# A four-layer streaming trunk on one core: order of work where a mixer joins its FFN, two squares on ScalarE, sums of squares inside the second gate unit

## What is computed

```python
for i in range(DEPTH):                       # DEPTH = 4
    h = _rmsnorm(x, attn_norm[i])
    if i % 3 == 0:   x = x + stick_breaking_mixer(h, ...)
    elif i % 3 == 1: x = x + mla_mixer(h, ...)
    else:            x = x + swa_sink_mixer(h, ...)
    x = x + swiglu_ffn(_rmsnorm(x, ffn_norm[i]), w_gate, w_up, w_down)
return _rmsnorm(x, final_norm)

def swiglu_ffn(h, w_gate, w_up, w_down):     # FFN_HIDDEN = 2816
    return (jax.nn.silu(h @ w_gate) * (h @ w_up)) @ w_down
```

## Time and profile before

| | |
|---|---|
| median of 3 runs | 1195.81 us (1195.05 to 1196.33) |
| profiled execution, own time | 1196.22 us |
| its span, first to last instruction | 1194.2 us |
| PE busy | 1168.3 us, 98% |
| PEld busy | 1040.5 us, 87% |
| DVE busy | 810.5 us, 68% |
| ACT busy | 628.3 us, 53% |
| POOL busy | 286.5 us, 24% |
| chain that ended last | PE 89%, DVE 8%, ACT 2% |
| mean granted clock of TensorE | 0.996 |

### The profile page before, as it was taken

How to read it: one execution, slowest core, us unless ns; L and a number is a source line. 1 busy time by engine, 2 the same in 40 slices (tenths; PEclk the granted TensorE clock), 3 DMA queues, 4 the chain that set the end, 5 groups by cost and what they waited for, 6 DMA issues and landing times.

```text
span 1194.2 us, 18227 instructions
## 1 busy us (share of the span) xinstructions
PE 1168.3 (98%) x7410; PEld 1040.5 (87%) x7410; DVE 810.5 (68%) x857; ACT 628.3 (53%) x763; POOL 286.5 (24%) x290
## 2 busy tenths in 40 slices
PE   8999999999999999999999999999999999999996
PEld 6988888888998888888899888888889888888885
DVE  7686767775588667776556577766556867777653
ACT  5675565554354555554436545555346755555531
POOL 5000542211123343221101153221110005422221
PEclk9999999999999999999999999999999999999999
DMA  9733545555552345555543245555545324455541
GB/s 314 217 121 106 176 177 180 180 206 194 186 174 89 114 160 212 180 182 206 194 156 107 82 170 212 183 201 201 187 160 193 106 106 177 177 193 187 196 165 35
DMA packets 30828, 201.84 MB, mean 169 GB/s; under 512 B 3504, under 2 KB 4592, under 8 KB 7328
## 3 DMA queue, kind: packets, MB, share of 16 engines
q1 hardware_dynamic: 28800, 197.41, 46.9%
q0 software_dynamic: 352, 1.31, 0.9%
q10 hardware_dynamic: 1600, 2.02, 0.7%
HBM read 197.91 MB, written 1.84 MB: 167 GB/s over the span
## 4 chain that ended last, share of the span: by engine, by line
PE 89%; DVE 8%; ACT 2%; DMA 0%; issue 0%; DVEq 0%; ACTq 0%
PE banks L1209 39%; PE banks L1213 21%; PE banks L1203 6%; PE banks L1205 6%; PE banks L1204 6%; PE banks L1197 4%; DVE w_lo L783 3%; DVE x_split L798 2%; PE banks L1338 1%; PE banks L1280 1%; PE banks L1352 1%; PE banks L1582 1%; DVE w_lo L792 1%; PE banks L1610 0%; ACT w_hi L458 0%; PE banks L1340 0%
## 5 line engine op out<-in xcount | busy, mean ns | idle before, releaser
L783 DVE TENSOR_TENSOR w_lo<-raw,w_hi 128x2048 fp32r<-128x2048 f32 x183 | 450.4, 2461 | 214.0 <-ACT w_hi L458 213.9
L458 ACT ACTIVATE w_hi<-raw 128x2048 fp32r<-128x2048 f32 x183 | 349.3, 1909 | 97.0 <-PE banks L1213 47.2
L1209 PE MATMUL banks<-x_split,w_hi 128*128 128x512 f32 x1408 | 339.1, 392 | 5.5 <-DVE x_split L798 5.4
L1209 PEld LDWEIGHTS banks<-x_split,w_hi 128*128 128x128 f32 x1408 | 258.6, 188 | 58.7 <-DVE x_split L798 8.9
L1213 PEld LDWEIGHTS banks<-x_split,w_lo 128*128 128x128 f32 x1408 | 181.8, 192 | 6.9
L1213 PE MATMUL banks<-x_split,w_lo 128*128 128x256 f32 x1408 | 184.0, 284 | 0.0
L1209 PE MATMUL banks<-hid_split,w_hi 128*128 128x512 f32 x704 | 173.2, 392 | 0.0
L1209 PEld LDWEIGHTS banks<-hid_split,w_hi 128*128 128x128 f32 x704 | 127.4, 188 | 23.3
L1203 PE MATMUL banks<-x_split,w_hi 128*128 128x256 f32 x384 | 110.3, 287 | 0.0
L1204 PE MATMUL banks<-x_split,w_hi 128*128 128x256 f32 x384 | 108.6, 283 | 0.0
L1205 PE MATMUL banks<-x_split,w_lo 128*128 128x256 f32 x384 | 108.6, 283 | 0.0
(11 more groups left out here) (174 smaller groups left out, 1476.9 us busy)
## 6 DMA issues: line engine op xcount, KB each, us to landing
raw<-w SPq DMA_DIRECT2D x183, 1024.0 KB, 4.9
raw<-w SPq DMA_DIRECT2D x8, 256.0 KB, 6.3
x<-x_in SPq DMA_DIRECT2D x2, 512.0 KB, 5.5
raw<-w SPq DMA_DIRECT2D x2, 512.0 KB, 8.4
out<-x SPq DMA_DIRECT2D x4, 256.0 KB, 2.9
k_all<-k_all ACTq DMA_DIRECT2D x1, 960.0 KB, 10.5
rel_scratch<-rel_lut POOLq DMA_DIRECT2D x1, 768.0 KB, 10.6
rel_bias<-rel_scratch POOLq DMA_DIRECT2D x2, 256.0 KB, 8.5
```

The lines of the kernel that those rows point to most:

```text
L458: act.activation(w_hi[slot][:, :], raw[slot][:, :], ACT.Copy).then_inc(hi_done, 1)
L783: dve.tensor_tensor(w_lo[slot][:, :], raw[slot][:, :], w_hi[slot][:, :].bitcast(FP32), ALU.subtract).then_inc(lo_done, 1)
L1209: return pe.matmul(pair(b), wt[0], xs, start=first, stop=False, skip_group_check=True)
```

## The change

It touches the join and the first two chunks of each FFN.

- VectorE, `out_projection`: the split of unit u+5 (b+1) moves from ahead of `norm_lo(n, 4)` to behind `norm_lo(n, 7)`.
- ScalarE, `out_projection`: behind the last split it squares tiles 6 and 7 of x into two free buffers and signals `two_squared`.
- GpSimd, `model_squares`, at the joins only (odd n): tiles 0 to 3 as before, 4 and 5 when all eight low parts are written, 6 and 7 are added from ScalarE's squares.
- TensorE: gate 0 goes in two runs, high and low matmuls of tiles 0 to 5, then of 6 and 7; `model_sums` moves from behind up 0 to between the high and the low matmuls of gate 1 (unit b+2).
- VectorE, first chunk: `up_sum(0)` ahead of `mean_square`.

```diff
+        late_squares = (ss[:, 1, :], rope_k[:, :])
...
                 tiles = KT if n < NORMS - 1 else KT - 1
                 for k in range(tiles):
+                    if n % 2 and k >= 6:
+                        pool.wait_ge(two_squared, n // 2 * 2 + k - 5)
+                        dst = sq_sum if k == 6 else ss[:, 0, :]
+                        ins = pool.tensor_tensor(dst[:, :], sq_sum[:, :], late_squares[k - 6], ALU.add)
+                        if k == 6:
+                            step(ins)
+                        else:
+                            ins.then_inc(norm.ss, 1)
+                        continue
                     if n == 0:
                         pool.wait_ge(x_loaded[k // 4], 16)
                     elif n < NORMS - 1:
-                        pool.wait_ge(norm.lo, 8 * n + k + 1)
+                        pool.wait_ge(norm.lo, 8 * n + (KT if n % 2 and k >= 4 else k + 1))
...
                 split(b + PAIRS - 1 + SPLIT_SLOTS)
+                for a in range(2):
+                    act.activation(late_squares[a], x[:, 6 + a, :], ACT.Square).then_inc(two_squared, 1)
...
                 add(4)
                 add(5)
-                split(u + SPLIT_SLOTS + 2)
                 norm_lo(n, 4)
                 norm_lo(n, 5)
                 add(6)
                 norm_lo(n, 6)
                 add(7)
                 norm_lo(n, 7)
+                split(u + SPLIT_SLOTS + 2)
                 split(u + SPLIT_SLOTS + 3)
...
                     if c == 0:
                         split(b + 3)
+                        up_sum(0)
                         mean_square(n)
-                        up_sum(0)
                         refine(norm, n + 1, 0, SEQ + TOKEN_SUMS[n], rstd)
...
-                def two_halves(u, first_bank, new):
+                def two_halves(u, first_bank, runs, new):
                     pe.wait_ge(lo_done, u + 1)
-                    for k in range(KT):
-                        if new:
-                            pe.wait_ge(norm.lo, 8 * n + k + 1)
-                        for a in range(2):
-                            high_halves(first_bank + a, w_tile(u % 3, a * KT + k), x_tile(k), k == 0)
-                    for k in range(KT):
-                        for a in range(2):
-                            last = low_half(first_bank + a, w_tile(u % 3, a * KT + k), x_tile(k), k == KT - 1)
+                    for run in runs:
+                        for k in run:
+                            if new:
+                                pe.wait_ge(norm.lo, 8 * n + k + 1)
+                            for a in range(2):
+                                high_halves(first_bank + a, w_tile(u % 3, a * KT + k), x_tile(k), k == 0)
+                        if u == b + 2:
+                            model_sums(n)
+                        for k in run:
+                            for a in range(2):
+                                last = low_half(first_bank + a, w_tile(u % 3, a * KT + k), x_tile(k), k == KT - 1)
                     last.then_inc(unit_used, 1)
...
-                    two_halves(b + 2 * c, GATE_BANKS[c % 2], c == 0)
+                    two_halves(b + 2 * c, GATE_BANKS[c % 2], (range(KT),) if c else (range(0, 6), range(6, KT)), c == 0)
...
-                    two_halves(b + 2 * c + 1, UP_BANKS[c % 2], False)
-                    if c == 0:
-                        model_sums(n)
+                    two_halves(b + 2 * c + 1, UP_BANKS[c % 2], (range(KT),), False)
```

More of the change, by code:

```diff
@@ L255, in trunk @@
         squared = sem("squared")
+        two_squared = sem("two_squared")
         scaled = sem("scaled")
```

## The result

The changed kernel takes 1197.01 us (median of 20 runs, 1196.83 to 1197.46), the kernel before 1195.12 us (20 runs, 1194.43 to 1196.75): ratio 1.0013, 95% interval 1.0007 to 1.0019. It is 0.13% slower. The time lies in the range given; the direction does not: 0.3 us faster was forecast, 1.9 us slower was measured. The slowest run of before (1196.75) is faster than the fastest of the changed kernel (1196.83), so the direction does not hang on the median.

A forecast was written before the change was run, and what follows sets the result against it. TensorE, busy 98% of the span, was taken to bound the kernel. Start of up 2 at four joins: 1.35 gained, then 0.14, 0.76 and 0.12 lost, together 0.33 us gained: 1195.9, or 1195.5 for the median; range 1192.6 to 1198.6.

The forecast's parts named there:

- 1.35 gained (this holds the 1.5 of the clock): First join, first FFN matmul to start of up 2: 31.85 us before, 30.50 after, with one clock fall of 1.5.
- 0.14 lost: Second join, first FFN matmul to start of up 2: 30.36 us before, 30.50 after.
- 1195.5 for the median: Whole kernel: 1195.9 us against the profiled execution's 1196.22, lowered because the median shown is 0.41 below that execution.
- the hand-off of the split of b+5: Before up 2: split ends 30.46 us after the first FFN matmul, hand-off at 30.50, TensorE waits 0.51.
- T + 10.0: GpSimd's last sum at a join, counted from the first FFN matmul (T): six operations, at worst two stretched to 2.56 us.
- Rival 1: Gain stays if the chain behind the sums fits in 7.9 us: 1186.6; chance 0.05, for a part 0.09.
- Rival 2: Clock falls at the new stalls, 1.5 us each: one fall gives 1197.0, two 1198.5, four 1201.5; chance 0.13.
- four like joins: Clock gate at the joins: one fall at four like joins, taken to agree with a free-running window.
- Rival 3: Split of b+1 comes too late for up 0; 1.4 us late at each join gives 1198; chance 0.05.
- Rival 4: At the joins tile 7 is still late, TensorE waits for the low parts as before: 1203; chance 0.01.
- The cost of nothing: At the joins: ScalarE's two squares, 0.42 us each, cost nothing; gate 0's two runs under 0.05 us; swapped up_sum nothing.

The follow-up runs named there:

- second trace: The kernel before, unchanged, in a further profiled execution: 1195.01 us.
- the one without the late wait: Changed kernel with the sums of squares behind up 0 and without GpSimd's wait for all eight low parts before squares 4 and 5: 1187.28 us.

## Why the prediction was wrong

**The mechanism was right.** No wait for L798, a new wait of 1.7 us before gate 2 and a second before up 2, four times each; the sums at T + 14.8; the chain of 9.63 us unchanged; gate 2 at T + 24.60 where T + 24.42 was given. The two single-part runs show it from both sides: the moved split alone gives 4 us, and the moved sums alone cost 10. Together they are the changed kernel, 2.4 us over the lower group and not 6, because 3.4 us of what the moved split could give is lost in waiting for GpSimd's sum, and with the sums at T + 14.8 that wait is not there.

**The step that failed is a term of the sum: the first join, "1.35 gained (this holds the 1.5 of the clock)".** It took the fall of the clock in the one profiled execution for a cost of the kernel. The three other traces of before have no fall at a join, and the groups of its run times put it into 9 of 20 runs. In the second trace up 2 starts at 161.60 - 131.20 = T + 30.40, so against T + 30.50 the first join loses 0.10 and gains nothing. With 0.14 lost there, as at the second join, my own sum gives 1.16 us slower instead of 0.33 faster. The sentence "The median of the runs shown is 0.41 below that execution, so 1195.5 for the median" carried the error on: the runs then shown (1195.05, 1195.81, 1196.33) were already of both groups.

**A second term was too small: the restart of a waiting TensorE.** The table shows it against the very trace of the forecast, with the fall in it: the four joins change by -1.08, +0.43, +1.04 and +0.40 us where -1.35, +0.14, +0.76 and +0.12 were given, 0.27 to 0.29 more each, 1.1 in all. So this term put right alone, with the fall left in, turns the direction too. Most of it is the hand-off of the split of b+5. I took 0.04 us behind the start of VectorE's next operation (15.67 to T + 30.50); it measured 162.29 - 162.07 = 0.22, which is 0.14 behind the recorded end of the split itself (159.86 + 2.29). At up 2 the changed kernel stands at T + 30.72, 0.22 behind the forecast, at four joins 0.9 us. The rest is the first pass after a stop, which is slower: behind up 2's stop 166.00 - 162.29 = 3.71 us against 3.65. The pass behind gate 2's stop took 159.93 - 156.17 = 3.76 at this join and 3.73 at the others, but TensorE stood idle behind it, so that it cost nothing. Gate 2 was given no hand-off at all and had 156.17 - (152.96 + 3.06) = 0.15.

**Third join.** In the first trace it lost 1.46 us in waiting; in the others the sums came at T + 12.28 in place of T + 12.60, and the stretch is 0.22 us shorter. Together 1.16 + 1.1 + 0.2 agree within 0.1 with the 501.65 - 499.23 = 2.42 us of the table, and with the 2.3 us between the changed kernel's median and the middle of the lower group (1194.7).

**GpSimd's time was wrong, without effect on the forecast.** "T + 10.0" was T + 12.75. Two stretched operations were an upper bound only for two splits beside them. There are three. It did no harm because the sums were wanted at T + 14.8; behind up 0 it costs 1.2 to 1.7 us a join, as the run with the sums moved back shows against the one without the late wait.

**The rivals.** Rival 1 (the gain stays) would have needed the chain 1.7 us shorter; it is unchanged. Rival 2 (the clock falls at the new stalls) did not occur: the profiled execution has 1.00 through all four new stalls, and the 20 runs lie within 0.63 us of each other, where before has 2.3. Of the "four like joins" three have the two gaps, and one of these had the fall; the third join has a single gap, of 0.83 us. Rival 3: the split of b+1 was in time. Rival 4: out, tile 7 was ready at 133.16 + 0.48, T + 2.07.

**The cost of nothing** held for ScalarE's squares (0.40 us each), for the two runs of gate 0 (0.03 us) and for VectorE's swapped up_sum.

## What to carry to other kernels

Before an event of one trace (a fall of the clock, a late transfer) enters a sum against a median, look whether the run times lie in groups that differ by its price; if they do, work the sum out with and without it. When a wait is removed, follow the chain behind every synchronisation point that is moved along with it: here a reduction put 3.65 us later on the engine that bounds the kernel made two weight splits late, because they stood behind it in the order of two other engines. An operation held back to keep out of another's way is only free if the time it finishes is still earlier than the first place where its result is wanted.

## What the runs showed of the hardware

Two gaps of 0.70 and 0.82 us within 2.3 us were followed by a fall of TensorE's granted clock to 0.50, the 1.2 GHz level, for some 3.4 us in one execution, and in three others with the same gaps at the same join they were not. Stops of 1.7 us before gate 2, four in each of the four kernels with the sums inside gate 1 and the split of b+4 in its old place, were followed by none. Near the start, where TensorE waits for the first low weight parts, three traces have a stop of 1.59 to 1.71 us and no fall, and the ten others one of 1.96 to 3.38 us and a fall.

GpSimd's elementwise operations of 0.61 to 0.81 us took 2.5 to 2.9 us when one of VectorE's splits of 2.3 us ran beside them, sums as well as squares; one that started when such a split had run for some time took 1.78. Where GpSimd's operation started first, VectorE's split became the longer one, 2.62 us in place of 2.29.

From the recorded end of a weight split to the first matmul of a TensorE that had stood waiting for it took 0.14 to 0.15 us.

What decides in which execution the clock falls at a join stays open.
